# A decoder layer on one core: where the second half's sums are taken in, ScalarE's order at the first MLP group, and the bank order of that group

## What is computed

```
y = jnp.concatenate([rmsnorm(y_mla, mla_out_norm_w[l]),
                     rmsnorm(y_nsa, nsa_out_norm_w[l])], axis=-1)
h = h + y @ w_o[l]
n = rmsnorm(h, mlp_norm_w[l])
h = h + jnp.square(jax.nn.relu(n @ w_up[l])) @ w_down[l]
return rmsnorm(h, final_norm_w)
```

## Time and profile before

| | |
|---|---|
| time, median of 3 runs | 1046.28 us (1045.77 to 1046.79) |
| the profiled execution's own time | 1042.38 us |
| its span | 1040.6 us |
| PE busy | 1019.8 us (98%) |
| PEld busy | 880.5 us (85%) |
| DVE busy | 792.9 us (76%) |
| ACT busy | 615.9 us (59%) |
| mean DMA rate | 183 GB/s |

### The profile page before, as it was taken

One profiled execution on the slowest core, in us unless ns is written; L12 is line 12 of the kernel. 1 busy time (PEld: TensorE's weight loads), 2 busy tenths in 40 slices (PEclk: granted clock), 3 DMA queues, 4 the chain that ended last, 5 costly groups with the idle time before them and its releaser, 6 DMA issues.

```text
span 1040.6 us, 14187 instructions
## 1 busy us (share of the span) xinstructions
PE 1019.8 (98%) x5547; PEld 880.5 (85%) x5547; DVE 792.9 (76%) x1086; ACT 615.9 (59%) x872; POOL 89.4 (9%) x151
## 2 busy tenths in 40 slices
PE   8999999999999999999999999999999999999997
PEld 7889999888888877888888888888888888888885
DVE  4655986988865589769958967976995896797594
ACT  5655856876754666456555655645655565565433
POOL 2135100633200000000000000000000000000002
PEclk9999999999999999999999999999999999999999
DMA  9576672342235546666666665666666666566553
GB/s 336 178 206 194 213 253 83 126 145 96 103 127 188 185 114 185 195 199 197 186 194 192 200 201 177 196 197 200 191 192 193 195 199 200 178 195 200 202 188 136
DMA packets 182798, 190.84 MB, mean 183 GB/s; under 512 B 9206, under 2 KB 145100, under 8 KB 182348
## 3 DMA queue, kind: packets, MB, share of 16 engines
q1 hardware_dynamic: 182300, 189.41, 58.1%
q10 hardware_dynamic: 432, 0.52, 0.1%
HBM read 187.82 MB, written 2.10 MB: 183 GB/s over the span
## 4 chain that ended last, share of the span: by engine, by line
PE 77%; DVE 11%; ACT 5%; DMA 4%; issue 3%; DVEq 0%; ACTq 0%
PE ps L2000 15%; PE ps L2004 8%; PE ps L2068 8%; PE ps L1559 4%; PE ps L1560 4%; PE ps L1563 4%; PE ps L2049 4%; PE ps L2075 4%; PE ps L2042 4%; PE ps L2043 4%; DMA raw<-in_w_up 4%; ACT high L826 2%; PE ps L1973 2%; DVE low L973 2%; PE ps L1850 2%
## 5 line engine op out<-in xcount | busy, mean ns | idle before, releaser
L973 DVE TENSOR_TENSOR low<-raw,high 128x2048 fp32r<-128x2048 f32 x120 | 259.4, 2162 | 57.9 <-ACT high L826 57.0
L826 ACT ACTIVATE high<-raw 128x2048 fp32r<-128x2048 f32 x120 | 217.3, 1811 | 133.8 <-DMA raw<-in_w_down 70.2
L2000 PE MATMUL ps<-xT,high 128*128 128x512 f32 x896 | 213.0, 390 | 1.7 <-DVE hid L1370 1.7
L2000 PEld LDWEIGHTS ps<-xT,high 128*128 128x128 f32 x896 | 168.0, 188 | 38.2 <-DVE hid L1370 2.6
L973 DVE TENSOR_TENSOR w_lo<-raw,w_hi 128x1024 fp32r<-128x1024 f32 (+4 forms) x79 | 129.5, 1644 | 66.9 <-ACT w_hi L632 66.0
L632 ACT ACTIVATE w_hi<-raw 128x1024 fp32r<-128x1024 f32 (+3 forms) x75 | 104.1, 1391 | 62.2 <-PE ps L1563 40.9
L2068 PE MATMUL ps<-high,hidT 128*128 128x512 f32 x544 | 135.1, 390 | 0.0
L2004 PEld LDWEIGHTS ps<-xT,low 128*128 128x128 f32 x896 | 114.9, 191 | 4.4
L2068 PEld LDWEIGHTS ps<-high,hidT 128*128 128x128 f32 x544 | 100.3, 188 | 19.7
L2004 PE MATMUL ps<-xT,low 128*128 128x256 f32 x896 | 116.2, 283 | 0.0
L2075 PE MATMUL ps<-low,hidT 128*128 128x512 f32 x272 | 72.7, 389 | 0.0
(11 more groups left out here) (367 smaller groups left out, 1893.9 us busy)
## 6 DMA issues: line engine op xcount, KB each, us to landing
raw<-in_w_up SPq DMA_DIRECT2D x64, 1024.0 KB, 6.3
raw<-in_w_down SPq DMA_DIRECT2D x36, 1024.0 KB, 5.2
raw<-in_w_down SPq DMA_DIRECT2D x56, 512.0 KB, 4.7
raw<-in_w_o SPq DMA_DIRECT2D x16, 1024.0 KB, 5.2
raw<-in_w_in SPq DMA_DIRECT2D x8, 1024.0 KB, 5.3
raw<-in_w_in SPq DMA_DIRECT2D x8, 816.0 KB, 4.4
raw<-in_w_in SPq DMA_DIRECT2D x6, 832.0 KB, 8.7
raw<-in_mla_w_uq SPq DMA_DIRECT2D x12, 256.0 KB, 4.6
```

Of the source, the lines that this page charges most:

```text
L826: act.activation(high4[:, n % RAW, c0:2048], raw[:, n % RAW, c0:2048], ACT.Copy).then_inc(done, 1)
L973: return dve.tensor_tensor(dst, src, high.bitcast(F32), ALU.subtract)
L2000: pe.matmul(ps[:, 0, :].rearrange("p (c t) -> p c t", c=2), high4[:, s, P * k:P * k + P], xT[:, :, k, :], start=k == 0, stop=False)
```

## The change

Four edits. (1) `half_add(g)` goes from the start of pair (g+1, 0) to pair (g, 7), between the first quad's weight sums and its low parts. (2) ScalarE at the first group: the high part of chunk 6 goes ahead of the squared ReLU of blocks 0 to 3 (VectorE's `hidden_parts(0, 0)` and `(0, 1)` go behind the low part of chunk 7 instead of chunk 6), the high part of up block (1, 1) ahead of the squared ReLU of blocks 4 to 7, and `up_copy(1, 0)` to the start of pair (1, 0). (3) VectorE at pair (1, 0) takes `up_add` ahead of `tile_sums_lo(0, 2)`. (4) `up_products` goes round its four banks: for each tile b all four blocks f, first with the high parts of the weights, then with the low ones; the sums are the same ones.

```diff
@@ ScalarE
                 if c == MLP0 + 5:
                     first_copy(0)
+                if c == MLP0 + 6:
                     square_relu(slice(0, 4), 1, first_sum, 1)
...
             first_copy(1)
+            up_weights_hi(1, 1)
             square_relu(slice(4, 8), 2, first_sum, 2)
             hidden_hi(0, 2)
             for g in range(1, G):
                 for i in range(8):
-                    if i < 7:
+                    if (g, i) == (1, 0):
+                        up_copy(1, 0)
+                    elif i < 7:
                         up_weights_hi(g, i + 1)
...
+                    if (g, i) != (1, 0):
+                        up_copy(g, i)
                     if i < 7:
                         down_weights_hi(g, i + 1)
...
-                    up_copy(g, i)
@@ VectorE
                 if c == MLP0 + 5:
                     first_add(0)
-                if c == MLP0 + 6:
+                if c == MLP0 + 7:
                     for p in range(2):
                         hidden_parts(0, p)
...
-                    if i == 0 and g > 1:
-                        half_add(g - 1)
...
-                    if i == 0 and g == 1:
-                        tile_sums_lo(0, 2)
...
                     up_add(g, i)
+                    if i == 0 and g == 1:
+                        tile_sums_lo(0, 2)
...
                     elif g < G - 1:
                         weight_sums(g + 1, 0)
+                        half_add(g)
                         down_weights_lo(g + 1, 0)
@@ TensorE, up_products
-                for f in range(4):
-                    if free is not None:
-                        free(f)
-                    both = ps[:, b0 + f, :].rearrange("p (c t) -> p c t", c=2)
-                    for b in range(4):
-                        pe.matmul(both, w_hi[:, slot, 512 * b + P * f:512 * b + P * f + P], xT[:, :, k0 + b, :],
-                                  start=start and b == 0, stop=False)
-                    for b in range(4):
-                        m = pe.matmul(ps[:, b0 + f, 0:T], w_lo[:, slot, 512 * b + P * f:512 * b + P * f + P], xT[:, 0, k0 + b, :],
-                                      start=False, stop=stop and b == 3)
+                for b in range(4):
+                    for f in range(4):
+                        if free is not None and b == 0:
+                            free(f)
+                        w = slice(512 * b + P * f, 512 * b + P * f + P)
+                        pe.matmul(ps[:, b0 + f, :].rearrange("p (c t) -> p c t", c=2), w_hi[:, slot, w], xT[:, :, k0 + b, :],
+                                  start=start and b == 0, stop=False)
+                for b in range(4):
+                    for f in range(4):
+                        w = slice(512 * b + P * f, 512 * b + P * f + P)
+                        m = pe.matmul(ps[:, b0 + f, 0:T], w_lo[:, slot, w], xT[:, 0, k0 + b, :], start=False, stop=stop and b == 3)
```

## The result

| | before | changed |
|---|---|---|
| time, median | 1045.77 us (5 runs, 1042.94 to 1046.79) | 1036.21 us (5 runs, 1036.18 to 1037.67) |
| ratio | | 0.9922, 95% interval 0.9907 to 0.9936 |
| the profiled execution's time, span | 1042.38, 1040.6 us | 1036.18, 1034.3 us |

Forecast were 1044.8 us and a range of 1042.6 to 1046.9. The measured time lies under the range. The two medians are 9.6 us apart, the ratio makes 8.2 us of it. Between the two profiled executions 6.3 us of the span went.

The account below looks back on a forecast made before the run. TensorE, busy 98% of the span, was taken to bound the kernel. First group +1.8 - 0.3 - 1.1 = +0.4 and six places -1.9 give -1.5 us: 1046.3 - 1.5 = 1044.8 us, range 1042.6 to 1046.9.

Parts of the forecast that it names:

- the chain in edit 1: At six places: `acc` stall of 1.14 us goes, `up_add` stays put, so only 0.42 arrives, net 0.31 us each.
- every gate that I listed: What TensorE waits for at the six places: the `acc` pair, then `t_low`, then `up_add` of pairs (3, 0) and (3, 1).
- Rival A: The six places give their stall back whole, VectorE being earlier in pair (g, 1): -5.7 us, 1040.6; chance 0.08.
- Edit 1: `half_add` ahead of the low parts: net 0.31 us at each of six places, -1.9 us.
- Edit 4, the waits: Chunk 0's third matmul wants bank 2 before it is free: TensorE stands 1.71 us plus 0.12 for restart, +1.8 us.
- The pace: Chunks 0 to 5 take 5.56 us instead of 5.60, 0.05 us gained on each: -0.3 us.
- rival D: Going round the banks slows every matmul of the eight chunks; at 20 ns each +2.3 us, 1048.6; chance 0.06.
- Edits 2 and 3: First group: chunk 6 starts without its wait, VectorE's list shortens, pair (1, 2) starts at 401.9 against 403.02: -1.1 us.
- The first group as a whole: Sum of the terms at the first group: +1.8 - 0.3 - 1.1 = +0.4 us.
- Rival E: Clock falls at the new stall or in the banks' round; a tenth of 45 us at half clock: 1049.3; chance 0.03.
- The carry-over: The median of the runs lies 3.9 us above the profiled execution; this difference was added to the forecast unchanged.
- rule on cycling through PSUM banks: Small idle moments between matmul groups swing the clock; the eight chunks could run partly at 1.2 GHz, many us worse.

Follow-up runs that it names:

- first series: The first four experiments, run with the kernel before beside them, whose median there was 1044.93 us.

## Why the prediction was wrong

**The step that failed** is the start of the chain in edit 1: "From the weight sums to `up_add` of pair (3, 0) VectorE does the same work as before without a pause, so that `up_add` stays where it was." The work is the same, but its start is not. The start hangs on `up_add(2, 7)`, for which VectorE waited on ScalarE's `up_copy`. I had read that edit as one of the first group, and so priced at nothing an edit that stands in 55 other pairs. Seen from the start of pair (3, 0)'s block, `up_add(2, 7)` began 554.88 - 552.95 = 1.93 us ahead before and begins 554.25 - 551.21 = 3.04 ahead now, and VectorE's wait for it shrank from 2.34 to 0.97. Those 1.1 us (0.9 to 1.5 over the six places) are enough to end every gate that I listed: `acc`, if left where it was, and `up_add(g, 1)`. The experiments bear out each half: without the early `up_copy` B shortens by 2.6, with it alone by 6.77, with it in one pair a group by 6.75.

**Rival A** had nearly the right size (-5.7 us, where from profile to profile 6.3 went) and the wrong cause: it looked for a pause hidden in VectorE's stretch. Inside the stretch there was only the 0.12 us behind the weight sums, too small for a bracket; the pause that counts stood ahead of it, in the bracket of the row at 552.95, which I had not shown among the rows.

**Edit 1** by itself was priced -1.9 and measures -2.80; the mechanism is the one described, the stall of 1.1 us gone and a wait for `hid` of 0.3 to 0.4 us come at (g, 2). Most of the 0.9 us between them is the 0.12 us at each of six places that VectorE saves when `acc` follows the weight sums: "stays where it was" was wrong by that much for this edit too.

**Edit 4, the waits**: +1.8 forecast; undoing it for chunk 0 gives 1.82. **The pace**: -0.3 forecast; the chunks are 5.56 to 5.57 apart from chunk 3 on. But chunks 1 and 2, which come behind transposes of `h_sb`, take 5.67 each, where they took 5.69 and 5.66, so that only about half of the 0.3 came. Going round the banks costs nothing, rival D is out. Waits and pace together measure +1.69 alone (+1.5).

**Edits 2 and 3**: chunk 6 without a wait, `up_add(1, 0)` and `(1, 1)` within 0.15 us as the sum of VectorE's list had it. No run has these two edits alone; taken off from the whole they are worth 0.50 - 1.69 = -1.2 (-1.1). The first group as a whole came to +0.5 (+0.4).

**Rival E**, the clock: the new stall of chunk 0 didn't bring the clock down in any trace read here. But the kernel before had a stall, of 1.98 us at chunk 6, behind which it fell in the one traced execution with the lower mean. The earlier trace rows come from an execution without it, and they could not have shown it: a 9 there is 90% or more, over a slice of 26 us, and the page of the execution with the fall has a 9 in each slice too. The clock across the stalls is read from shorter windows; from 331 to 381 the kernel before has 1.00 in the earlier trace rows's execution. Whether the change gains by taking that stall away is not shown: three kernels that keep it never had the lower mean clock, as the next section says.

**The carry-over** from the profiled execution to the median was wrong in kind too. I added a fixed 3.9 us. In the three series the runs of the kernel before fall in two bunches instead, around 1042.7 and around 1045, and the profiled one was of the lower. There 8 of 33 timed executions had a mean clock of 0.996, seven of them in the first series, and were about 2.5 us longer. The one trace of such an execution accounts for 1.56 us of that. The first five runs, up to 1046.79 us, have no clock on record, so what made them long is open. The changed kernel's median lay 0.03 us above its profiled execution, where I had added 3.9.

## What to carry to other kernels

When an engine works without a pause over a long stretch and gates others at its end, ask first what its start waits for: here some 1.1 us there at each of six places were worth 6.75 in all, and the order inside the stretch 2.8 by itself and nothing beside the earlier start. Read an edit's condition for the cases that it leaves in, `!= (1, 0)` as 55 pairs, and compare the instruction order at a second place before pricing. Going round accumulators asks for all of them within a few matmuls; keep the first round in blocks where one is still being read.

## What the runs showed of the hardware

- TensorE's granted clock fell to half for about 3.4 us behind a wait of 1.98 us in one execution of the kernel before (369.6 to 373), and stayed full behind the same wait in another. What decides between the two is open. All 14 runs of three other kernels with the same wait at chunk 6 (1034 to 1038 us of span) had a mean clock of 0.998 or 0.999, and so had the changed kernel's five. The lower mean was seen in 8 of 33 runs of the kernel before and, as 0.996 or 0.997, in seven of eleven of the bank order alone: the two kernels that have the wait at chunk 6 and the six waits for `acc`. Since the one fall that was traced comes over 100 us before the first wait for `acc`, that doesn't name a cause. A mean of 0.997 doesn't by itself mean a long run: the two runs of chunk 0 in the old order that had it were the shortest of the five.
- The Trainium skill, "TensorE: Matmul & The Clock Gate", section "HAM oscillation — how this bites in real kernels", tells of a clock that falls at gaps in which TensorE waits for loads. The trace agrees in kind: the fall stands behind a wait, here one for VectorE. The Trainium skill's rule on cycling through PSUM banks, which the prediction weighed, puts the fall down to small idle moments between groups of matmuls. Chunks 3 to 7 of the changed kernel follow each other without one, 5.56 us apart at the full clock, so going round four banks does not by itself bring the clock down here; what such idle moments would do no run shows.
- Sixteen matmuls over four banks in turn take the same 3.65 us as sixteen into one bank (352.40 to 356.05 in the bank order alone; 3.64 in the earlier trace rows).
